# Two attention blocks with experts on one core: the order of the gated linear attention's gate work, and the operands of the expert gating tables

## What is computed

```
def gla_mixer(h, w_in, w_g2, b_g2, norm_g, w_out):
    q, k, v, og, gl = split(h @ w_in)
    log_a = log_sigmoid(gl @ w_g2 + b_g2) / 16
    b = cumsum(log_a within a chunk)
    q_t = q * dk**-0.5 * exp(b);  k_t = k * exp(-b);  k_dec = k * exp(b_last - b)
    o = tril(q_t k_t^T) v + q_t S        # S, the state: S = diag(exp(b_last)) S + k_dec^T v
    o = rmsnorm(o, norm_g)               # over the 256 values of a head
    return (o * silu(og)) @ w_out        # silu(x) = x * sigmoid(x)

def peer(h, w_q, subkeys, u_tab, v_tab):
    e = i1 * 128 + i2 for the 16 best pairs of 8 heads;  g = softmax(their scores)
    a = gelu(h . u_tab[e]);  return sum(g * a * v_tab[e])
```

## Time and profile before

| | |
|---|---|
| median of 3 runs | 3434.97 us (3434.64 to 3437.86) |
| the profiled execution | 3433.47 us |
| its span | 3431.6 us, so 1.9 us lie around it |
| mean granted clock of TensorE | 0.951 |
| busy: PE, DVE, ACT, POOL | 3119.2, 1919.6, 1670.1, 1337.0 us |

### The profile page before, as it was taken

How to read it: one execution, slowest core, us unless ns; L and a number is a source line. 1 busy time by engine, 2 the same in 40 slices (tenths; PEclk the granted TensorE clock), 3 DMA queues, 4 the chain that set the end, 5 groups by cost and what they waited for, 6 DMA issues and landing times.

```text
span 3431.6 us, 58529 instructions
## 1 busy us (share of the span) xinstructions
PE 3119.2 (91%) x18424; PEld 2773.2 (81%) x18424; DVE 1919.6 (56%) x3062; ACT 1670.1 (49%) x3151; POOL 1337.0 (39%) x1068
## 2 busy tenths in 40 slices
PE   6957999997899998799999779999899989999998
PEld 6746999996677776689999767777678778999997
DVE  7443535009899992434700689999410423555555
ACT  1112477778644442437777774444312214555554
POOL 7200489886455550029988755555100000000000
PEclk6888999999999999899999999999999997999999
DMA  6412455550388873135555118877344233555553
GB/s 222 154 61 81 146 167 171 170 189 14 126 279 257 256 235 117 51 129 171 171 166 183 67 61 280 257 257 257 124 153 141 99 104 111 185 187 186 184 186 132
DMA packets 154590, 556.48 MB, mean 162 GB/s; under 512 B 17024, under 2 KB 19840, under 8 KB 154384
## 3 DMA queue, kind: packets, MB, share of 16 engines
q1 hardware_dynamic: 152288, 551.62, 49.0%
q10 hardware_dynamic: 2224, 3.87, 0.3%
HBM read 554.37 MB, written 1.05 MB: 162 GB/s over the span
## 4 chain that ended last, share of the span: by engine, by line
PE 43%; issue 28%; DVE 16%; POOL 6%; ACT 5%; DVEq 1%; ACTq 1%; POOLq 0%; PEldq 0%
PE bank L637 14%; PE bank L924 11%; PE bank L450 7%; PE bank L942 5%; POOL w_parts L2131 5%; DVE a_parts L1837 5%; DVE w_parts L1834 3%; DVE h_parts L1834 3%; ACT hT L1226 3%; DVE mean L1845 2%; DVE hT L1845 2%; ACT hT L1222 1%; POOL arena L2170 1%; PE bank L663 1%; PE bank L906 1%
## 5 line engine op out<-in xcount | busy, mean ns | idle before, releaser
L2131 POOL TENSOR_TENSOR w_parts<-ring,w_parts 128x512 fp32r<-128x512 f32 x512 | 686.3, 1367 | 596.9 <-ACT w_parts L1186 592.2
L637 PE MATMUL bank<-h_parts,w_parts 128*128 128x256 f32 x6144 | 745.5, 284 | 25.1 <-POOL w_parts L2131 23.0
L637 PEld LDWEIGHTS bank<-h_parts,w_parts 128*128 128x128 f32 x6144 | 741.3, 193 | 29.4 <-POOL w_parts L2131 26.5
L1186 ACT ACTIVATE w_parts<-ring 128x512 fp32r<-128x512 f32 x512 | 321.5, 630 | 203.8 <-PE bank L637 198.3
L2082 DVE TENSOR_TENSOR w_parts<-ring,w_parts 128x512 fp32r<-128x512 f32 x384 | 265.3, 692 | 245.1 <-ACT w_parts L1379 237.2
L663 PE MATMUL bank<-w_parts,a_parts 128*128 128x512 f32 x1536 | 372.0, 398 | 16.8 <-DVE a_parts L1837 16.8
L450 PE MATMUL bank<-hT,ring 128*128 128x256 f32 x1584 | 356.2, 388 | 29.1 <-ACT hT L1117 29.1
L663 PE MATMUL bank<-h_parts,a_parts 128*128 128x512 f32 x1536 | 367.3, 395 | 16.8 <-DVE a_parts L1837 16.8
L924 PEld LDWEIGHTS bank<-h_parts,w_parts 128*128 128x128 f32 x3072 | 375.2, 193 | 5.6 <-issue 3.3
L924 PE MATMUL bank<-h_parts,w_parts 128*128 128x256 f32 x3072 | 376.1, 284 | 2.6 <-DVE w_parts L2082 2.6
L1379 ACT ACTIVATE w_parts<-ring 128x512 fp32r<-128x512 f32 x384 | 242.0, 631 | 268.1 <-PE bank L924 177.2
(11 more groups left out here) (310 smaller groups left out, 4314.0 us busy)
## 6 DMA issues: line engine op xcount, KB each, us to landing
ring<-stream SPq DMA_DIRECT2D x882, 512.0 KB, 3.4
arena<-stream SPq DMA_DIRECT2D x168, 512.0 KB, 4.5
arena<-consts ACTq DMA_DIRECT2D x1, 1536.0 KB, 6.5
xT<-xin ACTq DMA_DIRECT2D x1, 1024.0 KB, 5.5
out<-hT SPq DMA_DIRECT2D x4, 256.0 KB, 2.2
arena<-subk ACTq DMA_DIRECT2D x2, 128.0 KB, 2.2
arena<-consts_s ACTq DMA_DIRECT2D x1, 256.0 KB, 2.6
cst<-consts ACTq DMA_DIRECT2D x1, 196.0 KB, 2.6
```

Of the source, the lines that this page charges most:

```text
L637: mm = pe.matmul(bank[k][:, 0:T], w[:, wp, ws], h_parts[:, hp, 4 * j + q, :], start=(j == 0 and q == 0 and i == 0), stop=(j == 1 and q == ...
L1186: act.activation(w_parts[half % HALVES][:, 0, :], ring[slot_][:, j * 512:(j + 1) * 512], ACT.Copy).then_inc(sem(f"{n}_high"), 1)
L2131: pool.tensor_tensor(w[:, 1, :], ring[(base + k) % RING][:, j * 512:(j + 1) * 512], w[:, 0, :].bitcast(F32), ALU.subtract).then_inc(sem(f" ...
```

## The change

On ACT, the wait for g_abs, the Sigmoid and the Ln move from behind the drains of v and og to the place ahead of them. The og tiles are drained with the function Silu in place of Copy, and so the sigmoid of og (L1155) and DVE's product with it (L1656) are gone. DVE multiplies og by the gain `gla_ng` in two instructions, behind the masks. The squares of heads 2 and 3 wait for PE's sum of squares of the head two before (`full_sem`), no longer for DVE's mean (`free_sem`). As soon as a head is squared, DVE multiplies its bank by og into G.o, ahead of the means; after the root it multiplies each head by the root, and signals g_y for each head, on which the output projection's first tile waits piece by piece.

In the table stage ACT's loop becomes 16 turns written out, with fixed columns. DVE first copies `iota` and the gates into bank 0, and ones2 and picked read them there.

```
@@ gla_pe
-            pe.wait_ge(sem("g_y"), 1)
-            project_norm(pe, "gla_out", G.o, "g_out", "0b")
+            project_norm(pe, "gla_out", G.o, "g_out", "0b", lambda q: (sem("g_y"), q // 2 + 1))
@@ gla_act
-            for nh in range(2):
-                for a in range(TT):
-                    copy_act(act, G.v[:, a, nh * 512:(nh + 1) * 512], f"g_v{nh}{a}", lambda t: t[:, :])
-            for c in range(8):
-                copy_act(act, G.og[:, c, :], f"g_og{c}")
             act.wait_ge(sem("g_abs"), 1)
             act.activation(G.e, G.e, ACT.Sigmoid, scale=-1.0).then_inc(signal("g_act"), 1)
             act.wait_ge(sem("g_act"), signalled("g_act"))
             act.activation(G.e, G.e, ACT.Ln).then_inc(signal("g_ln"), 1)
             act.wait_ge(sem("g_ln"), signalled("g_ln"))
-            act.activation(G.o, G.og, ACT.Sigmoid).then_inc(signal("g_sig"), 1)
-            act.wait_ge(sem("g_sig"), signalled("g_sig"))
+            for nh in range(2):
+                for a in range(TT):
+                    copy_act(act, G.v[:, a, nh * 512:(nh + 1) * 512], f"g_v{nh}{a}", lambda t: t[:, :])
+            for c in range(8):
+                copy_act(act, G.og[:, c, :], f"g_og{c}", func=ACT.Silu)
...
                 if h >= 2:
-                    act.wait_ge(free_sem(f"g_ss{h - 2}"), freed(f"g_ss{h - 2}"))
+                    act.wait_ge(full_sem(f"g_ss{h - 2}"), filled(f"g_ss{h - 2}"))
@@ peer_act
-            with act.Fori(0, T // TURN) as it:
+            for it in range(T // TURN):
...
-                        tok = bass.ds(it * TURN + s, 1)
+                        tok = slice(it * TURN + s, it * TURN + s + 1)
@@ gla_dve
-            dve.wait_ge(sem("g_sig"), 1)
-            dve.tensor_tensor(G.og, G.og, G.o, ALU.mult).then_inc(signal("dve_step"), 1)
-            dve.wait_ge(sem("dve_step"), signalled("dve_step"))
...
+            og4 = G.og.rearrange("p (h e) t -> p h e t", e=2)
+            dve.wait_ge(free_sem("g_og6"), freed("g_og6"))
+            dve.wait_ge(free_sem("g_og7"), freed("g_og7"))
+            for e in range(2):
+                dve.tensor_scalar(og4[:, :, e, :], og4[:, :, e, :], V("gla_ng")[:, e:e + 1], None, ALU.mult)\
+                   .then_inc(signal("dve_step"), 1)
...
+            dve.wait_ge(sem("dve_step"), signalled("dve_step"))
+            for h in range(GH):
+                dve.wait_ge(sem("g_sq"), h + 1)
+                ins = dve.tensor_tensor(G.o[:, 2 * h:2 * h + 2, :], bank[4 + h][:, :].rearrange("p (e t) -> p e t", e=2),
+                                        G.og[:, 2 * h:2 * h + 2, :], ALU.mult)
+            ins.then_inc(signal("dve_step"), 1)
             inv_root_dve(dve, "g", G.r, G.e2, [f"g_ss{h}" for h in range(GH)], GDV)
             for h in range(GH):
-                for e in range(2):
-                    dve.scalar_tensor_tensor(G.o[:, 2 * h + e, :], bank[4 + h][:, e * T:(e + 1) * T],
-                                                        V("gla_ng")[:, e:e + 1], G.r[:, h, :], ALU.mult, ALU.mult).then_inc(signal("dve_step"), 1)
-                    dve.wait_ge(sem("dve_step"), signalled("dve_step"))
-            dve.tensor_tensor(G.o, G.o, G.og, ALU.mult).then_inc(signal("g_y"), 1)
-            dve.wait_ge(sem("g_y"), signalled("g_y"))
+                dve.tensor_tensor(G.o[:, 2 * h:2 * h + 2, :], G.o[:, 2 * h:2 * h + 2, :],
+                                  G.r[:, h:h + 1, :].broadcast_to([P, 2, T]), ALU.mult).then_inc(signal("g_y"), 1)
@@ peer_dve
+            iota_p, gates_p = bank[0][:, 0:P], bank[0][:, P:P + T]
+            dve.tensor_copy(iota_p, iota)
+            dve.tensor_copy(gates_p, route[:, 2, :]).then_inc(signal("dve_step"), 1)
+            dve.wait_ge(sem("dve_step"), signalled("dve_step"))
...
-                dve.tensor_tensor(hot2[:, 4 * k:4 * k + 4, :], iota.unsqueeze(1).broadcast_to([P, 4, P]),
+                dve.tensor_tensor(hot2[:, 4 * k:4 * k + 4, :], iota_p.unsqueeze(1).broadcast_to([P, 4, P]),
...
-                dve.scalar_tensor_tensor(part, part, 0.0, route[:, 2, bass.ds(it * TURN + 4 * k, 4)].unsqueeze(2)
+                dve.scalar_tensor_tensor(part, part, 0.0, gates_p[:, bass.ds(it * TURN + 4 * k, 4)].unsqueeze(2)
```

## The result

The changed kernel takes 3376.8 us (median of four runs, 3375.2 to 3377.4). The kernel before, measured beside it, took 3435.9 us (3434.6 to 3437.9). The ratio is 0.9827, with a 95% interval of 0.981 to 0.9844. The time fell by 59.1 us, and by 58.3 us between the two profiled executions (3433.47 and 3375.16 us, span 3373.4), where the prediction had 54.3 us. The sign and the range were right; the sum was 4 to 5 us too small.

What follows compares the result with a forecast made beforehand. PE's waits on chains of other engines bounded the attention stage, and ACT paced the table stages. Attention 42.8 plus tables 11.5 made 54.3 us less, forecast 3381 us, range 3374 to 3392 (own range 3375 to 3386).

Steps and rivals of the forecast that it cites:

- Gate chain: Attention stage: activations moved early hide DVE's chain beside PE's projections; transposes start 35.8 us earlier, first chunk 1.5 more.
- Product ahead of the root: End of attention stage: multiplying by og before the root shortens PE's wait, 5.8 us gained, 0.3 lost, 5.5 net.
- Tables, 11.5 us foretold: Two gating-table stages: ACT's fixed columns cut each turn by 0.36 us to 6.70, saving 11.5 us (8.6 to 14.4).
- so 0.10 remains of it: Table turns: each ACT gap from Abs to Relu loses its 0.07 us register piece, leaving 0.10 of 0.17 us.
- DVE's 7.09 would be the next bound: it is the condition: Table stages: without operands in the bank, DVE's 7.09 us turn would bound and none of the 11.5 us remain.
- A: Rival, table stages: they give nothing, as DVE stays stretched by POOL or ACT's gaps stay; 3392 us, chance 0.12.
- B: Rival, end of attention stage: it gives nothing, products out of the banks taking 1.23 us; 3386 us, chance 0.08.
- C: Rival, attention stage: DVE's gate work is not hidden beside PE's projections; wholly in series 3418 us, chance 0.04.
- D: Rival, table stages: ACT's written-out code stalls on instruction supply; 3445 us at 2 us a turn, chance 0.03.

Runs made afterwards that it cites:

- gate chain alone: Kernel before with only ACT's early gate activations and Silu in the og drains; squares, root products and final product as before: 3398.7 us, ratio 0.9893.
- run with two groups on DVE from SBUF: Changed kernel with a second of each table turn's four groups given to DVE, which reads column numbers and gates from SBUF: 3430.3 us, ratio 0.9986.
- fixed columns run: Changed kernel with ACT's table loop and register waits back, every turn using the columns of the first 16 tokens: 3375.4 us in a single run.
- tables' own run: Kernel before with both table parts (ACT written out, DVE's operands in the bank) and the old attention stage: 3421.2 us, ratio 0.9956.
- longer chain: Changed kernel with 24 more DVE instructions, 30.2 us in all, computing an unread square before PE's transposes: 3389.4 us in a single run.
- last experiment: Two groups on DVE from the bank, but only one every second turn, DVE's and PE's table loops also written out: 3352.5 us, ratio 0.9758.

## Why the prediction came out right, and where its steps failed

**Gate chain, 35.8 + 1.5 = 37.3 us: right.** The first chunk is 37.5 us earlier, 37.2 without the 0.3 us from the start of the execution: 35.9 up to the first transpose and 1.3 from there on (4.27 − 2.95). The gate chain alone gives 36.7 us in time. DVE's chain ran beside PE's projections at its own durations (L1648 1.22 us, L1650 1.22 us), and its length to the decayed keys of 30.4 us (153.95 to 184.35) is close to the 30.5 foretold. The first transpose runs at a granted clock of 1.00, and no drain of v or og makes PE wait.

**Product ahead of the root, 5.5 us: right.** Between the first chunk and the output projection the kernel gains 5.5 us (37.5 to 43.0), just the sum, and its terms hold as well: 0.2 us lost up to the last mean (0.3 foretold), 5.7 gained behind it (15.2 − 9.5; 5.8 foretold). In the changed kernel's trace there are 0.9 us more: PE idled 4.95 us less (10.75, not 15.70), was back at the high level sooner, and the first tile was done 5.30 us after the start and not 6.17. One would like to book this to the shorter wait. The runs do not bear it out. One window each, about 2 us into the projection, of the kernel before, of the changed kernel and of the run with the attention part alone:

```profile
284.80:286.80 2.00, 2.00 (x6) 1.64 (x5) 0.00 (x0) 0.00 (x0) 0.00 (x0) 0.50 0.70 233
```

```profile
241.80:243.80 2.00, 2.00 (x8) 1.65 (x7) 0.00 (x0) 0.00 (x0) 0.00 (x0) 0.69 0.75 254
```

```profile
242.60:244.60 2.00, 2.00 (x6) 1.58 (x5) 0.00 (x0) 0.00 (x0) 0.00 (x0) 0.50 0.74 252
```

The last one has the short wait of 10.75 us and still the low clock, and its first tile takes 6.08 us. Over all traces the tile takes 5.27 to 6.08 us behind the wait of 10.75 (seven kernels) and 6.04 to 6.57 behind that of 15.70 (five). So a part of it may hang on the wait, but the 0.9 us are not shown to.

**Given back behind the stage: not an effect of the change.** 2.2 us (44.2 to 42.0) go again before the tables, 1.5 of them near 350 us. PE comes out of a wait there in both kernels, and the windows show it at different clocks, before (392 to 400 us) first:

```profile
392.00:400.00 8.00, 8.00 (x69) 8.00 (x68) 7.93 (x53) 6.11 (x9) 8.00 (x7) 1.00 0.52 169
```

```profile
349.00:357.00 8.00, 8.00 (x57) 8.00 (x56) 7.93 (x52) 4.92 (x8) 6.87 (x6) 0.80 0.49 152
```

But the same two clocks turn up the other way round. The run with DVE from the bank alone, which up to here is the kernel before, and the run with two groups on DVE from SBUF, which up to here is the changed kernel:

```profile
392.00:400.00 8.00, 8.00 (x56) 8.00 (x56) 7.93 (x53) 5.35 (x8) 6.62 (x6) 0.79 0.40 133
```

```profile
349.00:357.00 8.00, 8.00 (x68) 8.00 (x68) 7.93 (x52) 6.21 (x9) 8.00 (x7) 1.00 0.50 164
```

The piece of PE's work from 391.7 to 396.1 us takes 4.4 us in six of the twelve traces and 5.9 in the other six, with old and new attention stages among both. It is a difference between executions.

Behind the first table stage it falls the other way: 0.78 before and 1.00 after, and the lead grows by 9.0 us where the stage itself gives 7.3.

```profile
893.00:897.00 4.00, 2.98 (x12) 1.93 (x11) 3.68 (x7) 2.91 (x7) 0.00 (x0) 0.78 0.18 45
```

```profile
842.50:846.00 3.50, 2.21 (x13) 1.77 (x14) 2.03 (x4) 2.57 (x6) 0.00 (x0) 1.00 0.00 0
```

This one is read, not tested: no run moved the clock on purpose. The two nearly cancel, and that is luck: no row of the kernel before could have told them.

**Tables, 11.5 us foretold, 14.7 measured: the term was too small.** The step that failed is "so 0.10 remains of it". The gap fell to 33 ns, below the 70 ns that ACT's copies out of a bank show when they wait for themselves. The three gaps of a turn were 230, 165 and 165 ns in the mean and are 34, 34 and 33: together 0.46 us, and that is all that a turn saves (7.07 − 6.61). Foretold were 0.36, so 16 turns save 7.3 us a stage and not 5.8. The pieces of register work between the first Relus, for which the prediction allowed up to 0.09 us, cost nothing: the Relus start 0.400, 0.385 and 0.385 us apart in both kernels. A turn of 6.61 us lies just within the 6.6 to 6.8 foretold, and 14.7 us just above the 14.4 that ended the term's range. The fixed columns run shows that nothing else in the loop had a part.

**Tables, "DVE's 7.09 would be the next bound: it is the condition": wrong.** ACT written out alone kept a turn of 6.61 us and 12.6 us of gain, where by that step it had to keep none. I had taken the busy turn of an engine for the time it needs. Unstretched, DVE's instructions start 0.60 us apart, since each record of 0.68 reaches 0.08 us into the next; nine of them need 5.4 us, not the 6.1 of the prediction. All above was waiting inside the instructions, and part of it gave way when ACT came faster. The step did no harm, because the change had the bank in it anyway. As long as ACT paces, the bank is worth 0.5 us a stage (108.25 to 107.77).

The rule of the Trainium skill that stood beside that step (SBUF — State Buffer, "Who interferes with whom") is borne out in each duration: 692 ns at most with one SBUF operand, up to 1529 with two. The conclusion that I hung on it was wrong. It says what an instruction takes beside another, and not which engine bounds the stage. Where DVE bounds it, the same contention decides 75 us: stages of 134.9 us against 96.8 and 97.5.

**The rivals.** A is out by the tables' own run (14.3 us). B, the end of the stage, is out by the 5.5 us between the gate chain alone and the whole attention part. C, the chain not hidden, is out with a margin of 19 us, as the longer chain shows. D, stalls of the written-out code, is out for ACT: in each stage the 48 gaps between Abs and Relu are 33 to 34 ns. In the last experiment PE's and DVE's loops are written out as well; its first stage meets its sum, and its second does not, with no run to separate stalls from the low clock seen there. The Trainium skill (Runtime: NRT & Kernel Launch, "Instruction fetch mechanics") says that sequential code is fetched ahead; ACT's gaps of 33 ns agree.

The sum by what was measured, against 54.3: start 0.3, first chunk 37.2, to the output projection 5.5, its first tile and up to 330 us 1.2, given back −2.2, tables 14.7, behind the first tables 1.7, and −0.1 elsewhere: 58.3 us. The two attention terms are 42.7 us against 42.8 foretold, the tables are 3.2 us over theirs, and the remaining 0.9 us are differences of clock and start that were in no term.

## What to carry to other kernels

A full busy share says that an engine never rests, not that it has no room. Where another engine's accesses stretch its instructions, look for the shortest distance at which two of them start (0.60 us here, nine in a turn of 7.07), and count with it before calling the engine the next bound. Then give it work: moving one group of ACT's to DVE brought 21.9 us more than the change had. But take the stretch away first, since the same move without the bank made each stage 20 us longer than in the kernel before.

Where an instruction waits for its neighbour on the same engine, look for register work in the gap; it stands on the path in full. When a wait of PE goes away altogether, count the low clock behind it as well (1.3 to 2.0 us here). When it is only shortened, don't: here the gain was not to be told from the scatter. And before you explain a difference of a microsecond or two between two traces, see whether two traces of the same code differ by as much.

## What the runs showed of the hardware

- The register work of the columns costs more than its own record. ACTq's piece in the gap is 0.07 us, but the gap from Abs to Relu went from 165 or 230 ns to 33 with fixed columns, loop or no loop.
- DVE instructions of 128x512 float32 last 0.67 to 0.68 us each but start 0.594 to 0.602 us apart when nothing stretches them, so their durations add up to more than the time they take.
- Such an instruction takes the same time with one operand in PSUM as with both in SBUF and no neighbour: 676 and 677 ns at the least. Beside POOL's instruction only the latter stretches, up to 1529 ns, and POOL's own stretches with it, from 1038 up to 1533.
- The mean stretch is no property of the instruction. The ones took 1042 ns in the kernel before and 959 with ACT faster and DVE still busy without a pause, in turns that were 0.46 us shorter.
- PE's first work behind a wait of 10.9 or 35.8 us started at a granted clock of 0.50 and took 4.27 to 4.97 us where it takes 2.95 at 1.00. How soon the high level comes back differs between executions of the same code.
